# Third attention group's maps combined on GpSimd, with deeper buffers, and expert weights in six slots in the last layer

## What is computed

```
# group c: two softmax maps a head, combined before the product with v
p1 = softmax(q1 @ k1.T * scale); p2 = softmax(q2 @ k2.T * scale)
o  = (p1 - lam * p2) @ v
o  = rms_norm(o, norm_g) * (1.0 - lambda_init)
...
x = x + g1 * (concat(y_a, y_b, y_c, y_d) @ w_out)
h = rms_norm(x, ln2_g) * (1 + sc2) + sh2
x = x + g2 * hier_moe(h)      # 32 experts: (silu(h @ w_gate) * (h @ w_up)) @ w_down
```

## Time and profile before

| what | value |
|---|---|
| median of 3 runs | 1601.35 us (1600.17 to 1603.58) |
| profiled execution, own time | 1594.81 us |
| its span | 1593.0 us |
| busy PE / DVE / ACT / POOL, share of the span | 84% / 39% / 23% / 17% |
| DMA | 336.76 MB, mean 211 GB/s |
| chain that ended last, by engine | PE 70%, DVE 12%, ACT 7%, issue 5%, DMA 4% |
| group c's stage, layer 0 / layer 1 | about 318 to 384 us / 1078 to 1146 us |
| group b's stage, layer 0 / layer 1 | about 384 to 426 us / 1146 to 1189 us |
| experts, layer 1 | about 1292 to 1571 us |

### The profile page before, as it was taken

One profiled execution on the slowest core, in us unless ns is written; L12 is line 12 of the kernel. 1 busy time (PEld: TensorE's weight loads), 2 busy tenths in 40 slices (PEclk: granted clock), 3 DMA queues, 4 the chain that ended last, 5 costly groups with the idle time before them and its releaser, 6 DMA issues.

```text
span 1593.0 us, 18145 instructions
## 1 busy us (share of the span) xinstructions
PE 1338.2 (84%) x6748; PEld 759.2 (48%) x6748; DVE 617.1 (39%) x1442; ACT 364.6 (23%) x825; POOL 268.8 (17%) x248
## 2 busy tenths in 40 slices
PE   5899999987895798889969999998779769987862
PEld 1446556645542454444434665664454345544441
DVE  4734433477624222432262343246762432211111
ACT  1311024454401111112111202254440211110101
POOL 0201200000000343323210120000000125332321
PEclk8999999999997899999968999999999879999995
DMA  8810222645457599999651122143116668999954
GB/s 299 290 35 19 96 79 80 237 160 154 168 185 316 205 330 378 411 402 408 219 218 40 53 96 79 62 177 132 54 48 226 264 233 313 402 403 406 398 198 183
DMA packets 98609, 336.76 MB, mean 211 GB/s; under 512 B 28370, under 2 KB 33106, under 8 KB 73272
## 3 DMA queue, kind: packets, MB, share of 16 engines
q1 hardware_dynamic: 74712, 305.52, 49.3%
q0 software_dynamic: 15072, 16.85, 4.7%
q10 hardware_dynamic: 8736, 13.21, 2.4%
HBM read 324.08 MB, written 28.98 MB: 222 GB/s over the span
## 4 chain that ended last, share of the span: by engine, by line
PE 70%; DVE 12%; ACT 7%; issue 5%; DMA 4%; POOL 1%; SPq 1%; ACTq 0%; DVEq 0%; POOLq 0%
PE bank L495 65%; DMA big<-in_moe_w_down_dram 2%; PE bank L773 2%; ACT pr_r L1404 2%; PE bank L870 2%; DVE pr_r L2067 2%; ACT pr_r L1451 1%; DVE pr_r L1935 1%; DVE pr_r L2070 1%; DMA big<-in_ada_w_dram 1%; PE bank L610 1%; DVE pr_r L1720 1%; DVE big L1676 1%; DVE small L1919 1%; DVE pr_r L1918 1%
## 5 line engine op out<-in xcount | busy, mean ns | idle before, releaser
L495 PE MATMUL bank<-big,pr_r 128*64 128x256 f32 (+2 forms) x3192 | 453.1, 403 | 88.4 <-issue 26.4
L495 PEld LDWEIGHTS bank<-big,pr_r 128*64 128x64 f32 (+1 forms) x3192 | 273.5, 152 | 239.9 <-issue 113.4
L495 PE MATMUL bank<-big,ht_r 128*128 128x512 f32 (+3 forms) x832 | 308.0, 555 | 1.9 <-ACT ht_r L1417 1.9
L495 PEld LDWEIGHTS bank<-big,ht_r 128*128 128x128 f32 (+1 forms) x832 | 143.8, 189 | 137.3 <-issue 126.0
L495 PE MATMUL bank<-big 128*128 128x256 f32 (+4 forms) x496 | 168.9, 478 | 18.5 <-DVE big L1860 5.7
L1591 POOL DMA_INDIRECT x_rows<-ht_r,slot_i x64 | 102.0, 1593 | 326.0 <-DVE ht_r L2073 312.4
L2067 DVE TENSOR_TENSOR pr_r<-pr_r,bank 64x256 f32<-64x256 f32 x65 | 27.5, 423 | 256.2 <-ACT pr_r L1451 238.4
L495 PEld LDWEIGHTS bank<-big 128*128 128x128 f32 (+2 forms) x496 | 91.6, 197 | 61.5 <-issue 29.7
L1451 ACT ACTIVATE pr_r<-bank 64x256 f32<-64x256 f32 x64 | 24.1, 377 | 410.8 <-PE bank L495 410.8
L1527 POOL TENSOR_SCALAR small<-small 128x1 f32<-128x1 f32 (+2 forms) x20 | 10.1, 504 | 598.2 <-DVE small L1899 336.5
L2073 DVE SCALAR_TENSOR_TENSOR ht_r<-bank,mix_r,mod 128x512 f32<-128x512 f32 x65 | 48.8, 751 | 132.6 <-PE bank L495 132.6
(11 more groups left out here) (298 smaller groups left out, 1215.0 us busy)
## 6 DMA issues: line engine op xcount, KB each, us to landing
big<-in_moe_w_gate_dram SPq DMA_DIRECT2D x63, 1024.0 KB, 14.7
big<-in_moe_w_up_dram SPq DMA_DIRECT2D x63, 1024.0 KB, 20.9
big<-in_moe_w_down_dram SPq DMA_DIRECT2D x63, 1024.0 KB, 25.5
big<-in_ada_w_dram SPq DMA_DIRECT2D x16, 3072.0 KB, 11.5
big<-in_w_in_dram SPq DMA_DIRECT2D x4, 3072.0 KB, 11.1
big<-in_w_out_dram SPq DMA_DIRECT2D x4, 2048.0 KB, 8.7
mod<-in_ada_b_dram SPq DMA_DIRECT2D x12, 512.0 KB, 10.1
big<-in_w_in_dram SPq DMA_DIRECT2D x2, 2048.0 KB, 8.1
```

The source lines that it names most:

```text
L495: return nc.tensor.matmul(o, l, r, start=start, stop=stop)
```

## The change

- K o on DVE ends with `kap` and raises a new semaphore, `kap_ready`. GpSimd (POOL) does the combination in two operations: `prob[m2] = kap * prob[m2]` (L1570 in the new numbering) and, after a wait for that, `prob[m1] = prob[m1] + prob[m2]` (L1571).
- `prob` has 6 places instead of 4 and moves to `ht_r`, `probT` 4 instead of 2.
- In group c scores are issued up to two maps further ahead, and in all groups PV o-2 instead of PV o-1 follows T o.
- In layer 1 the experts use all six slots in turn; `OVER_SLOT` is 0 in both layers.

```diff
-        prob, probT = at(pr_r, 0, 4, S), at(pr_r, 2048, 2, S)
+        PB, TB = 6, 4
+        prob, probT = at(ht_r, 2 * S, PB, S), at(pr_r, 0, TB, S)
...
-                while given < min(v[3][-1] + 3, len(maps)):
+                while given < min(v[3][-1] + (5 if v[0] == "c" else 3), len(maps)):
                     steps.append(("S", given))
                     given += 1
                 steps.append(("T", o))
-                if o:
-                    steps.append(("PV", o - 1))
+                if o >= 2:
+                    steps.append(("PV", o - 2))
...
-        EXPERT_SLOT = [2, 3, 0, 1, 4, 5] + [(2, 3, 0, 1)[i % 4] for i in range(NE - 6)]
+        SIX = (2, 3, 0, 1, 4, 5)
+        EXPERT_SLOTS = [list(SIX) + [SIX[i % 4] for i in range(NE - 6)], [SIX[i % 6] for i in range(NE)]]
...
-        OVER_SLOT = [3] * DEPTH
+        OVER_SLOT = [0, 0]
...
+                for o in range(NH * NT):
+                    m1_, m2_ = outs[A_MAPS + o][3]
+                    g.wait_ge(kap_ready, NH * NT * l + o + 1)
+                    step(g.tensor_scalar(prob[:, m2_ % PB, :], prob[:, m2_ % PB, :], kap[:, o:o + 1], None, ALU.mult))
+                    g.tensor_tensor(prob[:, m1_ % PB, :], prob[:, m1_ % PB, :], prob[:, m2_ % PB, :], ALU.add).then_inc(diff_ready, 1)
...
-                            step(TS(kap[:, o:o + 1], rs[:, m1_:m1_ + 1], neglam, mx[:, m2_:m2_ + 1], ALU.mult, ALU.mult))
-
-                            STT(out=prob[:, m1_ % 4, :], in0=prob[:, m2_ % 4, :], scalar=kap[:, o:o + 1],
-                                in1=prob[:, m1_ % 4, :], op0=ALU.mult, op1=ALU.add).then_inc(diff_ready, 1)
+                            TS(kap[:, o:o + 1], rs[:, m1_:m1_ + 1], neglam, mx[:, m2_:m2_ + 1], ALU.mult, ALU.mult).then_inc(kap_ready, 1)
```

More of the change, by code:

```diff
@@ L398, in trunk @@
                     steps.append(("P", mods[o]))
-            steps.append(("PV", len(outs) - 1))
+            steps += [("PV", len(outs) - 2), ("PV", len(outs) - 1)]
             steps_of.append(steps)
@@ L431, in trunk @@
                 chunk_at[l, c] = (i, loaded[i])
-            for e, i in enumerate(EXPERT_SLOT):
+            for e, i in enumerate(EXPERT_SLOTS[l]):
                 loaded[i] += 48
@@ L436, in before_in_slot @@
         def before_in_slot(e):
-            return max((n for n in range(e) if EXPERT_SLOT[n] == EXPERT_SLOT[e]), default=None)
+            slots = EXPERT_SLOTS[in_layer[0]]
+            return max((n for n in range(e) if slots[n] == slots[e]), default=None)
         def last_in_slot(s):
-            return max(n for n in range(NE) if EXPERT_SLOT[n] == s)
+            return max(n for n in range(NE) if EXPERT_SLOTS[in_layer[0]][n] == s)
         def chunk_slot(c):
@@ L772, in layer @@
                         for j in range(nb):
-                            last = nc.tensor.transpose(b[:, j * P:(j + 1) * P], prob[:, ms[0] % 4, j * P:(j + 1) * P], ident[:, :])
+                            last = nc.tensor.transpose(b[:, j * P:(j + 1) * P], prob[:, ms[0] % PB, j * P:(j + 1) * P], ident[:, :])
                         last.then_inc(ready_a, 1)
@@ L786, in layer @@
                                  "c": cols_c[:, kt, 512 + h // 2 * P:512 + (h // 2 + 1) * P]}[g]
-                            last = mm(b[:, 0:P], probT[:, n % 2, j * P:(j + 1) * P], v, j == 0, j == len(tiles) - 1)
+                            last = mm(b[:, 0:P], probT[:, n % TB, j * P:(j + 1) * P], v, j == 0, j == len(tiles) - 1)
                         last.then_inc(ready_v, 1)
@@ L881, in expert @@
                 def expert(e):
-                    b, s = e % 2, EXPERT_SLOT[e]
+                    b, s = e % 2, EXPERT_SLOTS[l][e]
                     pe.wait_ge(xt_ready, NE * l + e + 1)
@@ L1098, in load_first @@
                 def load_first(e):
-                    s = EXPERT_SLOT[e]
+                    s = EXPERT_SLOTS[l][e]
                     wg, wu, _ = expert_slot(s)
@@ L1211, in layer @@
                     sp.nop()
+                last_in_0 = last_in_slot(0)
                 in_layer[0] = l + 1
@@ L1220, in layer @@
                 if l + 1 < DEPTH:
[L1221 removed]
+                    sp.wait_ge(y_done, NE * l + last_in_0 + 1)
                     load_chunk(IN[1], l + 1)
@@ L1392, in layer @@
                         g, h, qt, m = maps[n]
-                        if n >= 4:
-                            done(act, f"T{out_of[n - 4]}")
+                        if n >= PB:
+                            done(act, f"T{out_of[n - PB]}")
                         if g == "b":
@@ L1409, in layer @@
                         b = R.take(f"T{n}")
-                        if n >= 2:
-                            done(act, f"O{n - 2}")
-                        A_(probT[:, n % 2, 0:w], b[:, 0:w], ACT.Copy).then_inc(taken_a, 1)
+                        if n >= TB:
+                            done(act, f"O{n - TB}")
+                        A_(probT[:, n % TB, 0:w], b[:, 0:w], ACT.Copy).then_inc(taken_a, 1)
                     elif what == "P":
```

9 lines of the change are left out of this document (5 added, 4 removed).

## The result

The changed kernel takes 1642.83 us (median of 4 runs, 1641.82 to 1645.52), the kernel before on the same chip 1600.76 (1595.60 to 1603.58). The ratio is 1.0269, with a 95% interval of 1.024 to 1.0298: it is slower by about 42 us, where I had forecast 13 less.

The account below looks back on a forecast made before the run. TensorE holds most of the chain, but group c is a closed chain through DVE and group b mostly DVE-bound; +30.8 - 11.0 - 10.8 - 22.4 = -13.4 us, so 1588.0 for 1601.35, range 1575 to 1605.

Parts of the forecast that it names:

- Part 1: Group c, combination on POOL: link 2.06 us instead of 0.80, +1.26 a step, +30.8 us together.
- behind a P: Group c, six transposes behind a P: their 5.26 us step is set by PE and doesn't move.
- the 26 steps that pay: Group c, both layers: 26 of 32 transposes each pay the longer link, 26 x 1.26 = +32.8 us.
- POOL dearer: Rival, group c: product 1.27 and sum 1.65, link 3.06 us; total +15.8, 1617 us; chance 0.12.
- the clock falls: Rival, group c: longer PE waits lower TensorE's clock, +39 us, total +26, 1627 us; chance 0.05.
- The chain stays closed: Group c: K still waits for a PV behind transposes that wait for POOL; step 3.53 becomes 4.79 us.
- Part 2: Group b: more scores issued early under POOL's links and less idle time, 5.5 us a layer, -11.0 us.
- One PV less before the first T: Before group c's first transposes in each layer: one PV less on PE, 1.0 us each, -2.0 us.
- Part 3: End of layer 0: waves and weights earlier, -8.4 us, and 2.4 for the clock after, -10.8 us together.
- Part 4: Experts of layer 1: earlier loads through six slots and earlier over block weights, -22.4 us together.
- over block: End of layer 1: weights right behind expert 31's, -10.0 us; its 32 products at better clock, -2.8 us.
- the slots: Layer 1, experts 10 and 11: six slots keep the load queue from running dry, -9.6 us.

Follow-up runs that it names:

- `e_pool_only`: Kernel before with only the combination moved to POOL in two operations, old order, places and slots: 1681.91 us, ratio 1.0563.
- `e_open_pool`: Changed kernel with K of the next output put ahead of PV o-2, combination still on POOL in two operations: 1569.71 us, ratio 0.9814.
- Parts 3 and 4 alone: Kernel before with only the new expert slots and OVER_SLOT 0: 1567.08 us, ratio 0.9797.
- `after`: The changed kernel itself, with the whole change against the kernel before: 1642.83 us, ratio 1.0269.
- `e_forms`: Changed kernel with four forms of POOL's product in turn by output: constant, repeated column as second array, copy, column over 256 columns; no kernel time given.
- `e_no_pool`: Changed kernel with the combination back on DVE in one operation, the rest of the change kept: 1554.32 us, ratio 0.9771.
- `e_no_product`: Changed kernel without POOL's product, so POOL only adds: 1574.08 us, ratio 0.989.
- `e_tt`: Changed kernel with POOL's product written as a product of two arrays, the factor's column repeated: 1621.16 us, ratio 1.0177.
- `e_fill`: Changed kernel with four extra overwritten products on PE ahead of each wait for POOL, except behind a P: 1616.45 us, ratio 1.0155.

## Why the prediction was wrong, point by point

**The step of the sum that failed is the link of Part 1.** "I take 0.65, the memset's rate for 512 columns plus 0.2" measured 1.565. It lies even above my upper bound of 1.27, "as dear as two inputs": no row of the trace supported that one input can't be dearer than two. The other terms of the link were right: the sum 1.27 (1.265 measured), the wait between them 0.09, the end 0.05 (0.06). What the link lacked was 0.10 from the end of K to POOL's start. What it costs by itself shows in a step of the changed kernel in which the granted clock was 1.00:

```profile
393.39 0.66 PE L777 MATMUL bank<-ident,ht_r 128*128 128x128 f32 x4
...
399.03 0.66 PE L777 MATMUL bank<-ident,ht_r 128*128 128x128 f32 x4 [2.79 <-POOL ht_r L1571]
```

That is 5.64 us (as in three steps of `e_pool_only` that begin with transposes of 0.66, 5.65 each): 2.11 more than the 3.53 before, not 1.26, and 0.38 more than the 5.26 behind a P, which I had left unchanged. Of the 26 steps that pay, 24 lie in the two stretches of group c: 24 x 2.11 + 6 x 0.38 = 53 us, where my term has 24 x 1.26 = 30. That is 23 of the miss.

**The clock was the larger half.** I dismissed it with "2.2 is nearer to 0.91 than to 9.36, and PE works more than half of each step". Both are true and neither was an argument: the two rows said nothing on where between them the clock falls. PE waited 2.0 to 3.4 us in nearly all steps, and the clock was 0.74 and 0.66. Group c is longer by 83.3 - 53 = 30 us than the link alone explains; the run with PE kept at work puts it at 23 to 29. The run without the product shows the clock falling in part with waits of at most 1.7 us, so at my own link of 2.06 some of it would probably have gone as well. At which waits it falls stays open: in `e_open_pool` it was 1.00 from 1100 to 1143 us through waits of 1.0 to 1.6 us, and in the step above the transposes behind a wait of 2.79 still took 0.66.

**The rivals.** "POOL dearer" (0.12) and "the clock falls" (0.05) both came. I had priced them apart, +60 for all of Part 1 with the dear product and +39 on top of Part 1 for the clock, and took them for independent. They are not: the longer the link, the longer PE waits. The mechanism of the first was also wrong. Nothing contended with POOL. All 32 products are within 13 ns of each other, with DVE reading PSUM beside some of them. The Trainium skill (SBUF — State Buffer, section Who interferes with whom) has DVE contend with POOL's reads when it has two inputs in SBUF or runs in a 2-port mode. DVE's operations over whole maps in group c read a bank of PSUM, so by that rule there is no contention here, and the trace agrees. Its cycle accounting (GPSIMD Engine Reference, section Elementwise — side-by-side cycle accounting) has the one-input body as the cheap one; the trace shows the contrary for this product, 1.565 against 1.265 us.

**What held.** The chain stays closed, in the order that I gave, and the deeper order hides none of the link. Part 2: -11.0 forecast, -9.7 in the trace. "One PV less before the first T" did not show (+1.7 in layer 0). Part 3: -8.4 forecast up to layer 1's first products, -7.7 measured. Its other 2.4, for the clock behind their start, belongs to the next stretch, which is 2.7 shorter; the products themselves show 1.0 of it, 15.67 instead of 16.64. Part 4: -22.4 forecast, -17.2 in the trace: over block -10.0 and its clock -2.8 as forecast (-10.1, -2.7), the slots -4.4 instead of -9.6. Parts 3 and 4 alone, as a kernel, gave -32 us against -33.2. In the terms of the profiled execution the miss is 1642.5 - 1581.4 = 61 us: 53 of it in group c, and 7 in Parts 2 to 4, which gave 37.3 instead of 44.2.

## What to carry to other kernels

Before moving work off a chain to an engine that is idle, ask whether the chain is closed through it: the place of K in DVE's order decided over 5% (1.0269 to 0.969) with the same two operations on POOL. The engine decided 5.0% in the order of the change, and next to nothing when each engine had the order that suits it. An operation without a row of its own kind and size in the trace has no upper bound from rows of other kinds; measure it first, in several forms. Where a change lengthens TensorE's waits in a stage at full clock, count the fall of the clock as part of the same case.

## What the runs showed of the hardware

- On GpSimd (`after` and `e_forms`) a product of 128x512 float32 with a column took 1.565 us, with a constant 1.493, as a product with the column repeated as a second array 1.040, a copy 0.611, and the sum of two full arrays 1.265.
- In group c the granted clock of TensorE was 1.00 with PE waits of 0.91 us in most steps (before), 0.98 and 0.94 with 0.81 and one or two longer ones (`e_no_pool`), 0.92 and 0.95 with 0.3 to 2.0 (`e_open_pool`), 0.91 and 0.81 with 0.3 to 1.7 (`e_no_product`), 0.73 and 0.68 with 1.4 to 2.8 (`e_tt`), 0.74 and 0.66 with 2.0 to 3.4 in nearly all steps (the change), and 1.00 again when extra products filled the same waits (`e_fill`). Those products, whose results are overwritten, made the kernel 18 us faster.
